# Second mixer: three gate projections on a normalised input, in 512-column matmuls with spill and sum

## What is computed

```python
u = rms_norm(h, attn_pre_norm[l])
proj = jnp.einsum("bsd,dc->bsc", u, w_in)
q, k, v, x_lru, g_lru, gate_attn, gate_lru = jnp.split(proj, list(SPLITS), axis=-1)
...
y_attn = attn @ w_branch_attn
y_lru = (hl * jax.nn.gelu(g_lru)) @ w_branch_lru
merged = jax.nn.sigmoid(gate_attn) * y_attn + jax.nn.sigmoid(gate_lru) * y_lru
return merged @ w_out
```

## Time and profile before

| what | us |
|---|---|
| median of 3 runs (1000.53 to 1000.98) | 1000.87 |
| the profiled execution | 1000.9 |
| its span, first to last instruction | 999.1 |
| PE busy | 992.0 |
| DVE busy | 736.6 |
| ACT busy | 620.4 |
| POOL busy | 269.2 |

### The profile page before, as it was taken

One profiled execution on the slowest core, in us unless ns is written; L12 is line 12 of the kernel. 1 busy time (PEld: TensorE's weight loads), 2 busy tenths in 40 slices (PEclk: granted clock), 3 DMA queues, 4 the chain that ended last, 5 costly groups with the idle time before them and its releaser, 6 DMA issues.

```text
span 999.1 us, 18897 instructions
## 1 busy us (share of the span) xinstructions
PE 992.0 (99%) x6276; PEld 886.3 (89%) x6276; DVE 736.6 (74%) x1138; ACT 620.4 (62%) x1134; POOL 269.2 (27%) x249
## 2 busy tenths in 40 slices
PE   9999999999999999999999999999999999999998
PEld 7899888889999898888898888899999988888886
DVE  7997777786667788788766799677877778774443
ACT  7555666665556767666654588966485578764332
POOL 2441223221212222222221137602031445441000
PEclk9999999999999999999999999999999999999999
DMA  9775555545553235555455454654444536556531
GB/s 329 249 309 180 186 193 185 190 177 191 190 179 128 86 130 208 188 190 189 169 194 205 171 178 165 209 199 140 165 169 168 182 115 215 206 171 205 173 125 43
DMA packets 37709, 180.88 MB, mean 181 GB/s; under 512 B 3472, under 2 KB 7824, under 8 KB 19984
## 3 DMA queue, kind: packets, MB, share of 16 engines
q1 hardware_dynamic: 37504, 179.99, 51.3%
q10 hardware_dynamic: 144, 0.08, 0.1%
HBM read 179.01 MB, written 1.05 MB: 180 GB/s over the span
## 4 chain that ended last, share of the span: by engine, by line
PE 97%; ACT 1%; DVE 1%; issue 0%; POOL 0%; POOLq 0%; ACTq 0%
PE bank L484 37%; PE bank L490 26%; PE bank L486 8%; PE bank L488 8%; PE bank L526 4%; PE bank L527 4%; PE bank L528 4%; PE bank L607 1%; PE bank L731 1%; PE bank L715 1%; PE bank L745 0%; PE bank L596 0%; PE bank L614 0%; PE bank L951 0%; PE bank L506 0%
## 5 line engine op out<-in xcount | busy, mean ns | idle before, releaser
L1479 DVE TENSOR_TENSOR wlo<-raw,whi 128x1024 fp32r<-128x1024 f32 (+1 forms) x289 | 355.8, 1231 | 71.1 <-ACT whi L984 68.4
L484 PE MATMUL bank<-xa,whi 128*128 128x512 f32 x1248 | 398.0, 396 | 0.5 <-DVE xa L1943 0.5
L984 ACT ACTIVATE whi<-raw 128x1024 fp32r<-128x1024 f32 (+2 forms) x289 | 301.4, 1043 | 85.1 <-PE bank L490 79.5
L490 PEld LDWEIGHTS bank<-xa,wlo 128*128 128x128 f32 x1664 | 301.5, 189 | 49.8
L490 PE MATMUL bank<-xa,wlo 128*128 128x256 f32 x1664 | 344.7, 279 | 0.0
L484 PEld LDWEIGHTS bank<-xa,whi 128*128 128x128 f32 x1248 | 194.6, 189 | 6.6 <-issue 0.6
L1015 ACT ACTIVATE spill<-bank 128x256 f32<-128x256 f32 x191 | 72.9, 382 | 147.1 <-PE bank L490 146.5
L1515 DVE TENSOR_TENSOR z<-bank,spill 128x256 f32<-128x256 f32 x184 | 77.4, 421 | 63.7 <-ACT spill L1015 62.9
L486 PE MATMUL bank<-xa,whi 128*128 128x256 f32 x416 | 113.9, 292 | 0.0
L488 PE MATMUL bank<-xa,whi 128*128 128x256 f32 x416 | 109.8, 282 | 0.0
L2035 POOL TENSOR_TENSOR gate<-act,rbc 128x256 f32<-128x256 f32 x44 | 64.2, 1458 | 169.1 <-ACT act L1144 164.0
(11 more groups left out here) (228 smaller groups left out, 1448.2 us busy)
## 6 DMA issues: line engine op xcount, KB each, us to landing
raw<-in_stream SPq DMA_DIRECT2D x137, 1024.0 KB, 4.8
raw<-in_stream SPq DMA_DIRECT2D x42, 512.0 KB, 4.8
raw<-in_stream SPq DMA_DIRECT2D x8, 768.0 KB, 4.3
bias<-in_bias SPq DMA_DIRECT2D x1, 3072.0 KB, 13.0
raw<-in_stream SPq DMA_DIRECT2D x8, 256.0 KB, 5.5
x<-in_x SPq DMA_DIRECT2D x4, 256.0 KB, 5.4
out<-x SPq DMA_DIRECT2D x3, 256.0 KB, 2.4
cons<-in_cons SPq DMA_DIRECT2D x1, 576.0 KB, 9.1
```

Source lines behind the costliest of these rows:

```text
L484: pe.matmul(dst, whi[:, slot, at + i, :], X[:, k, :, :], start=first and i == 0, stop=False)
L490: ins = pe.matmul(narrow, wlo[:, slot, at + i, :], X[:, k, 0, :], start=False, stop=last and i == len(tiles) - 1)
L984: act.activation(whi[:, p, 0:kts, :].rearrange("p k m -> p (k m)"), src, ACT.Copy)\
L1479: dve.tensor_tensor(wlo[:, p, 0:kts, :].rearrange("p k m -> p (k m)"), src, whi[:, p, 0:kts, :].rearrange("p k m -> p (k m)").bitcast(F32) ...
```

## The change

`g2`, `ga` and `gl` become wide segments: they are entered in `S0`, PE runs them with 512-column matmuls, ACT spills, and DVE uses `sum_tile` in place of `scale_tile`. A sum of two halves and a multiplication by `rbc` would be two DVE instructions; so that one is enough, the input is multiplied by `rbc` beforehand. That input is made in `rg` and `v2`: DVE multiplies x by gain and `rbc` into `gl`, used as scratch (two tiles at each of r = 24 to 27, ahead of the weights), POOL rounds the tiles into `xb` behind its rotations, and DVE subtracts to get the lo part (one tile at each of r = 28 to 35, behind the weights). PE waits for all eight lo tiles before r = 36. Since `xb` is now in use until `gl` is done, the head outputs go to `xa`, the recurrence output to `xb` and the merged branches to `xa`.

```diff
+            def normed_input(k):
+                dve.scalar_tensor_tensor(out=gl[:, k, :], in0=x[:, k, :], scalar=vec("pre2", k), in1=rbc[:],
+                                         op0=ALU.mult, op1=ALU.mult).then_inc(xn_ready, 1)
+
+            def normed_input_lo(k):
+                dve.wait_ge(xn_hi, k + 1)
+                dve.tensor_tensor(xb[:, k, 1, :], gl[:, k, :], xb[:, k, 0, :].bitcast(F32), ALU.subtract)\
+                   .then_inc(xn_lo, 1)
...
                 if name == "rg":
+                    normed_input(2 * (r - AT["rg"]))
+                    normed_input(2 * (r - AT["rg"]) + 1)
                     next_weights(n)
...
                     next_weights(n)
+                    normed_input_lo(r - AT["v2"])
...
-                        scale_tile(n, r, dst)
+                        sum_tile(S0[name] + t, r % 4, dst)
...
+            for k in range(KT):
+                pool.wait_ge(xn_ready, k + 1)
+                pool.wait_ge(piece_done, R0 + AT["rg"] + (3 if k < 4 else 4))
+                pool.tensor_copy(xb[:, k, 0, :], gl[:, k, :]).then_inc(xn_hi, 1)
             pool.wait_ge(xc_lo, KT)
...
-                    blocks(r % 4, xa, range(8), acc(r, segment_of(r) in S0), True, True).then_inc(piece_done, 1)
+                    if r < AT["rg"]:
+                        blocks(r % 4, xa, range(8), acc(r, True), True, True).then_inc(piece_done, 1)
+                    else:
+                        if r == AT["g2"]:
+                            pe.wait_ge(xn_lo, KT)
+                        blocks(r % 4, xb, range(8), acc(r, True), True, True).then_inc(piece_done, 1)
...
-            first_body("ba", xb, None, att_lo, PAIRS1, IN_ORDER)
-            rest("ba", xb)
-            first_body("bl", xa, None, lru_lo, 0, STAIR)
-            rest("bl", xa)
-            first_body("out2", xb, None, mrg_lo, 0, STAIR)
-            rest("out2", xb)
+            first_body("ba", xa, None, att_lo, PAIRS1, IN_ORDER)
+            rest("ba", xa)
+            first_body("bl", xb, None, lru_lo, 0, STAIR)
+            rest("bl", xb)
+            first_body("out2", xa, None, mrg_lo, 0, STAIR)
+            rest("out2", xa)
```

More of the change, by code:

```diff
@@ L63 @@
 _s = 0
-for _name in ("bx", "up0", "dn0", "up1", "dn1", "x2", "q2", "k2", "ba", "out2", "mup"):
+for _name in ("bx", "up0", "dn0", "up1", "dn1", "x2", "q2", "k2", "g2", "ga", "gl", "ba", "out2",
+              "mup"):
     S0[_name] = _s
@@ L272, in build @@
         projected = sem("projected")
+        xn_ready = sem("xn_ready")
+        xn_hi = sem("xn_hi")
+        xn_lo = sem("xn_lo")
         rot_out = sem("rot_out")
@@ L1320, in beside @@
                     act.wait_ge(att_out, PAIRS1 + i + 1)
-                    act.activation(xb[:, i, 0, :], bank[OUT][:, 0:TOK], ACT.Copy).then_inc(att_hi, 1)
+                    act.activation(xa[:, i, 0, :], bank[OUT][:, 0:TOK], ACT.Copy).then_inc(att_hi, 1)
                 if head_of(r - 4) is not None:
@@ L1362, in _ @@
                         act.wait_ge(lru_ready, k + 1)
-                        act.activation(xa[:, k, 0, :], xc[:, k, :], ACT.Copy).then_inc(lru_hi, 1)
+                        act.activation(xb[:, k, 0, :], xc[:, k, :], ACT.Copy).then_inc(lru_hi, 1)
                 if t == 1:
@@ L1368, in merged_hi @@
                 act.wait_ge(merged, t + 1)
-                act.activation(xb[:, t, 0, :], z[:, t % 4, :], ACT.Copy).then_inc(mrg_hi, 1)
+                act.activation(xa[:, t, 0, :], z[:, t % 4, :], ACT.Copy).then_inc(mrg_hi, 1)
             for t in range(8):
@@ L1852, in beside @@
                     dve.wait_ge(att_hi, PAIRS1 + i + 1)
-                    dve.tensor_tensor(xb[:, i, 1, :], bank[OUT][:, 0:TOK], xb[:, i, 0, :].bitcast(F32),
+                    dve.tensor_tensor(xa[:, i, 1, :], bank[OUT][:, 0:TOK], xa[:, i, 0, :].bitcast(F32),
                                       ALU.subtract).then_inc(att_lo, 1)
+            def normed_input(k):
[5 more added lines that the diff above has]
+                   .then_inc(xn_lo, 1)
             for r in range(AT["ba"]):
@@ L1876, in _ @@
                         dve.wait_ge(tables_ready, 2)
-                    if name in S0:
+                    if r < AT["rg"]:
                         j = r - AT["q2"]
@@ L1900, in _ @@
                         dve.wait_ge(lru_hi, k + 1)
-                        dve.tensor_tensor(xa[:, k, 1, :], xc[:, k, :], xa[:, k, 0, :].bitcast(F32), ALU.subtract)\
+                        dve.tensor_tensor(xb[:, k, 1, :], xc[:, k, :], xb[:, k, 0, :].bitcast(F32), ALU.subtract)\
                            .then_inc(lru_lo, 1)
@@ L1905, in merged_lo @@
                 dve.wait_ge(mrg_hi, t + 1)
-                dve.tensor_tensor(xb[:, t, 1, :], z[:, t % 4, :], xb[:, t, 0, :].bitcast(F32), ALU.subtract)\
+                dve.tensor_tensor(xa[:, t, 1, :], z[:, t % 4, :], xa[:, t, 0, :].bitcast(F32), ALU.subtract)\
                    .then_inc(mrg_lo, 1)
```

## The result

The change made the kernel slower. The median of four runs is 1007.11 us (1006.53 to 1007.84) against 1000.91 (1000.53 to 1000.98) of the kernel before: a ratio of 1.0063, with a 95% interval from 1.0051 to 1.0075. The profiled execution took 1006.53 us with a span of 1004.5, which is 5.4 more than the span before. Two single runs of this study, one of e4 (1205.61 us) and one of the kernel before (3459.62 us), lie far above the others of the same kernel and are left out of the ranges and ratios.

The account below looks back on a forecast made before the run. PE was taken to bound the kernel, busy 992.0 of 999.1 us. On 1000.9 us: gain -2.25, wait +5.0, branch start +0.1, clock +1.5, sum +4.35, giving 1005.2 us, range 1001.8 to 1008.6.

Parts of the forecast that it names:

- The likeliest case: Before the first gate piece: DVE comes late and PE's clock falls in the pause; chance 0.50, 1005.2 us.
- The new wait: Before r = 36 PE waits for the lo part of tile 7: 3.1 least plus 1.9 lateness, 5.0 us, bounds 3.1 and 7.3.
- DVE's lateness: At the value banks of r = 35: added subtractions, meetings with POOL and a delay, less 3.4 us of pauses; 1.9 us taken.
- The 0.6 us of delay at r = 27: The added products of x, gain and statistic delay DVE's weights at r = 27 by 0.6 us; PE does not feel it.
- The clock: Behind the new pause PE runs at half pace for a while: +1.5 us, the middle of 0 and 3.0.
- The gain: In the 24 gate pieces, two wide matmuls per tile for three narrow ones save 0.093 us a piece, -2.25 us in all.
- The spill in the gate pieces: ACT's spill of some 0.3 us per gate piece starts DVE's chain later; put at nothing, 6.7 us if uncovered.
- The start of the branch: At the attention branch projection (`ba`), one spill ahead of ACT's rounding delays head 7's lo part by 0.28: about +0.1 us.
- The signs: Expected in the profile: one PE wait, about 5 us; banks 1.9 late; POOL's products ending near 649; granted clock below 1.00.
- a clock that stays up: Rival 1: DVE is late but PE's clock does not fall in the pause; 1003.7 us, chance 0.25.
- not late: Rival 2: between r = 28 and 35 DVE's pauses swallow everything added; wait 3.1, 1001.8 us, chance 0.15.
- Weight loads as the pace: Rival 4: PE's weight loads set the narrow gate pieces' pace, so fewer loads make it faster; some 983 us, chance 0.02.

Follow-up runs that it names:

- e4: The kernel before with g2, ga and gl wide and nothing prepared; DVE adds halves and multiplies by the statistic in two instructions: 999.83 us, ratio 0.9991.
- e2: The changed kernel with POOL's eight products of the recurrence held back until the first gate piece is done: 1004.60 us, ratio 1.0039.
- e1: The changed kernel with the lo parts of tiles 6 and 7 both made at r = 34, ahead of that piece's weights: 1000.98 us, ratio 1.0001.
- e3: The changed kernel with twelve matmuls of constants, result unread, put ahead of PE's wait before the first gate piece: 1004.66 us, ratio 1.0039.
- e6: The kernel before with wide gates, nothing prepared, two DVE instructions, and the last head rounded and subtracted ahead of the weights of r = 59: 998.96 us, ratio 0.9979.
- e8: The changed kernel with narrow gate projections (3 matmuls of 256 columns, no ACT spill, DVE copies), the prepared input and PE's wait kept: 1008.06 us, ratio 1.0072.
- e7: The changed kernel with lo tiles 6 and 7 at r = 34, POOL's products behind the first gate piece, last head before r = 59's weights: 999.21 us, ratio 0.9983.
- e5: The changed kernel with POOL's products held back until the first gate piece is done and twelve matmuls of constants ahead of PE's wait: 1004.61 us, ratio 1.0036.
- e9: The changed kernel with POOL's products held back until the first gate piece is done and seven matmuls of constants ahead of PE's wait: 1003.54 us, ratio 1.0027.

## Why the prediction was right, and where it was off

The forecast was 1005.2 us in a range from 1001.8 to 1008.6, slower; measured are 1007.11 and, in the profiled execution, 1006.53. The likeliest case is the one that came: DVE late, and the clock falls. The place, the order of the waits and the sign are right; that the sum is as near as 1.1 us to the profile is in part luck, as the steps show:

- **The new wait, 5.0.** 4.91. Its least part was put at 3.1: e2, without lateness, waits 3.3. DVE's lateness was put at 1.9: 1.74. Its cause is shown by e2, in which only the time of POOL's products differs and the lateness is gone, and the products were where the prediction put them, from 639.61 to 648.90. That the value banks ahead of the last subtraction make up the rest is shown by e1. Inside the lateness two errors nearly cancel. The 0.6 us of delay at r = 27 did not come: those weights start at 638.12, which is to 0.02 the 637.72 of the earlier trace rows and the 0.42 by which everything is later. And DVE used only 2.8 of its 3.4 us of pauses. Between these weights and the value banks DVE needs 19.08 us where it was 17.36: its additions are 4.5, in place of 5.0, and 1.7 of them are left. That the value banks would not pay for POOL, since they read PSUM, stood on rows in which no product ran beside them (POOL's end at 643.64, the banks start later); the changed kernel shows it, 0.74 us from 648.22 with a product running up to 648.90. One bank was met and six other instructions, not two and six.
- **The clock, +1.5.** It fell, as it had at the end of the program. Read from two profiles of the same program it costs 1.40 and 2.73 us; by medians of e3 and the changed kernel 2.4. The middle of the bounds was on average too low by 0.9, and by medians this is the largest error of the sum. A single value was the wrong form for a term that differs from run to run; the bounds, 0 and 3.0, held. The upper one came from comparing 634 ns at the start of the program with 0.28 us of another kind of matmul (float32r operands); matmuls of full float32 operands with 256 columns, as at the start, take 379 ns in e3 at 2.4 GHz. They are slow at the start even so, though the profile's clock column reads 1.00 there.
- **The gain, -2.25.** -1.91 (e4 and e6). The mis-sized term is the 0.093 a piece: it came from pieces with nothing between them (times 24 it is 2.23), and beside attention steps each wide piece is shorter by 0.08 to 0.09 only (the pairs 5.66 for 5.83, where the prediction said 5.57 for 5.76). This explains 0.2 of the missing 0.34.
- **The spill in the gate pieces, nothing.** Right: no wait of PE there in any kernel, with one more DVE instruction a piece in e6 and DVE busy 71.76 of 79.42 us.
- **The start of the branch, +0.1.** 0.35, the step that failed in its working though it is small. The DVE instruction that gives `lo` of head 7 came 0.46 us later, not 0.28: the spill is 0.28 of it, and the weights ahead of it took 1.45 us instead of 1.26, probably in its turns with POOL's third group of products, which runs at this place in both kernels (730.91 to 739.48 before, 736.19 to 744.75 now) and is met at another moment. Timelines of DVE and PE:

```profile
742.01 1.45 DVE L1488 TENSOR_TENSOR wlo<-raw,whi 128x1024 fp32r<-128x1024 f32 x1 [0.52 <-ACT whi L993]
743.38 0.41 DVE L1862 TENSOR_TENSOR xa<-bank,xa 128x256 fp32r<-128x256 f32 x1
```

```profile
743.43 0.27 PE L494 MATMUL bank<-xa,wlo 128*128 128x256 f32 x1
743.84 0.50 PE L488 MATMUL bank<-xa,whi 128*128 128x512 f32 x1
```

- **The signs.** The wait, the late value banks (1.74 us), the place of POOL's products and the low clock came as written. One sign of being wrong came too: gate pieces take longer than 2.8 us (2.83 to 2.98 in e6, with no wait of PE). It was badly set, as it took the pace of pieces with nothing between them for pieces beside attention steps.
- **What the sum had not.** The start of the program (+0.42) is of no kernel: it scatters by 0.7 us between profiles. The end (+0.26) is of some: see the last section.

Against the sum's +4.35 the profile reads +5.43: pause -0.09, gain +0.34, clock -0.10, branch +0.25, start +0.42, end +0.26.

Of the rivals, a clock that stays up (1003.7) is what e3 makes by hand, at 1004.66; "not late" is e2, but even there the wait alone (3.3 us) let the clock fall, which that rival had left out: its 1001.8 came out as 1004.60. The price of a wait under 4 us was thus under-told, and the point at which the kernel is slower by more than 0.2% lies below the wait of 4.15 us named there. Weight loads as the pace: excluded by e4, e6 and e8.

## What to carry to other kernels

A step that prepares an operand must end ahead of every instruction that waits for the consumer's previous piece; look at what stands before its last part in the list of the producing engine, since two short instructions behind such a wait cost 6 us here. A pause of the matrix engine costs more than its length if the clock falls for it: here pauses of 3.3 and 4.9 us cost 1 to 3 us on top in most runs, and one of 0.9 us nothing. Before an operand is prepared to save one instruction a piece, see whether the engine has room for that instruction: here it had, and the version with two instructions (e6) is as fast as the mended change (e7), with less work.

## What the runs showed of the hardware

**The clock.** With PE idle for 4.91 us (the changed kernel) and 3.3 us (e2) it fell from 2.4 to 1.2 GHz; with 0.9 us (e1) it didn't, nor where matmuls of constants filled the pause (e3, e5, e9). The Trainium skill (TensorE: Matmul & The Clock Gate, section HAM oscillation — how this bites in real kernels) has waits of the matrix engine between groups of matmuls as what throttles it, so that it starts the next group cold. These rows agree.

I had not expected that the same pause costs different amounts in the same program (1.40 and 2.73 us). Part of the scatter goes with it: e2's runs at a mean clock of 1.000, 0.998 and 0.996 took 1003.26, 1004.50 to 1004.66 and 1006.16 us. In the first of them the clock can't have been low for long, so a pause of 3.3 us does not always bring the fall.

**DVE and POOL.** Beside the first group of products an instruction of DVE that reads two tiles in SBUF takes about 0.55 us longer, whatever its size (0.41 becomes 0.96, 1.21 becomes 1.76); beside the third group one of 1024 columns took 1.45. The scaling of the value banks, which reads PSUM, takes 0.74 with and without POOL. A product takes 0.73 alone and up to 1.78 beside DVE.

**The end of the program.** From the start of the last matmul to the last instruction are 3.85 to 3.88 us in the kernel before, e4 and e6, and 4.12 to 4.14 in the eight kernels that prepare the input. The difference lies between the last two semaphore instructions of POOL, behind all work, whose starts are 0.1 us apart before and 0.4 in the changed kernel (first and last start in the rows, before and after):

```profile
L112 POOLq EVENT_SEMAPHORE  x2: 17/17/17, 998.9 to 999.0; - x2
L113 POOLq EVENT_SEMAPHORE  x2: 17/17/17, 1004.0 to 1004.4; - x2
```

I have not tested which part of the preparation does it, and the cause is open.
